# Column tiles for the SSM lag and V products and for the sample value products of the second layer

## What is computed

```python
def s5_scan(u, h0, ...):                       # layer 0, 96 groups of 16 channels, 64 states
    a_bar, b_bar = jnp.exp(lam_dt), ((a_bar - 1.0) / lam)[..., None] * bmat
    # h[t] = a_bar * h[t-1] + b_bar @ u[t];  y[t] = real(cmat @ h[t]) + d * u[t]

def stick_breaking_attention(q, k, v, q_offset):   # layer 1, 12 heads of 128
    z = jnp.einsum('bqhd,bkhd->bhqk', q_blk, k).astype(jnp.float32) * scale
    log_keep = jnp.where(causal, jax.nn.log_sigmoid(-z), 0.0)
    later = lax.cumsum(log_keep, axis=3, reverse=True) - log_keep
    w = jnp.where(causal, jnp.exp(jax.nn.log_sigmoid(z) + later), 0.0)
    return jnp.einsum('bhqk,bkhd->bqhd', w.astype(v.dtype), v)

def layer_b(x, k_all, v_all, q_offset, mk, mv, w_in, w_out, g_pre, g_post):
    q, gate, mq, mg = _split_proj(rms_norm(x, g_pre) @ w_in)
    b_out = stick_breaking_attention(...) * jax.nn.silu(gate)
    m_out = mem_attention(mq, mk, mv) * jax.nn.silu(mg)
    return x + rms_norm(jnp.concatenate([b_out, m_out], axis=-1) @ w_out, g_post)
```

## Time and profile before

| | |
|---|---|
| median of 3 runs | 2393.51 us (2393.07 to 2394.95) |
| profiled execution | 2395.48 us, span of the trace 2393.9 us |
| PE busy | 2296.2 us (96%) |
| DVE, ACT, POOL busy | 1014.2, 892.0, 237.0 us |
| chain that ended last | PE 78%, DVE 10%, DMA 4%, issue 4%, ACT 3% |

### The profile page before, as it was taken

The page is one execution under the profiler, slowest core; times in us unless marked ns, Lnnn a source line. Parts: engine busy times, 40 slices in busy tenths (PEclk is TensorE's granted clock), DMA queues, the critical chain, the costliest instruction groups (busy, mean ns, idle before and its releaser), DMA issues.

```text
span 2393.9 us, 35551 instructions
## 1 busy us (share of the span) xinstructions
PE 2296.2 (96%) x13685; PEld 2074.6 (87%) x13685; DVE 1014.2 (42%) x1775; ACT 892.0 (37%) x1637; POOL 237.0 (10%) x479
## 2 busy tenths in 40 slices
PE   8999999999799999999999999999999999889997
PEld 6799999999788998887888889988989988878886
DVE  5658877987534463225221222222211223543223
ACT  5533333334345352224222223544445444442221
POOL 1520000000101000002000000111121111010001
PEclk9999999999999999999999999999999999989999
DMA  7634453534534334224233334334343345344223
GB/s 257 219 87 103 103 110 92 115 95 99 203 115 146 106 103 167 77 73 158 93 101 101 100 93 140 103 112 138 99 132 114 103 147 197 100 144 166 79 78 133
DMA packets 197626, 293.38 MB, mean 123 GB/s; under 512 B 48324, under 2 KB 126672, under 8 KB 194096
## 3 DMA queue, kind: packets, MB, share of 16 engines
q1 hardware_dynamic: 158832, 166.80, 24.6%
q0 software_dynamic: 19856, 81.51, 10.3%
q10 hardware_dynamic: 18864, 44.05, 5.1%
HBM read 243.75 MB, written 48.55 MB: 122 GB/s over the span
## 4 chain that ended last, share of the span: by engine, by line
PE 78%; DVE 10%; DMA 4%; issue 4%; ACT 3%; POOL 0%; SPq 0%; ACTq 0%; DVEq 0%; POOLq 0%
PE PS L206 11%; PE PS L1336 11%; PE PS L1338 11%; PE PS L1337 11%; PE PS L207 11%; PE PS L208 10%; DVE WL L188 2%; PE PS L1122 1%; PE PS L489 1%; DVE FA L642 1%; DVE FA L638 1%; PE PS L792 1%; DVE FA L633 1%; PE PS L1107 1%; DVE FA L635 1%
## 5 line engine op out<-in xcount | busy, mean ns | idle before, releaser
L206 PE MATMUL PS<-XH,WH 128*128 128x320 f32 x2336 | 742.1, 318 | 3.7 <-DVE XL L1405 1.4
L207 PE MATMUL PS<-XL,WH 128*128 128x320 f32 x2336 | 725.3, 311 | 0.0
L208 PE MATMUL PS<-XH,WL 128*128 128x320 f32 x2336 | 725.0, 310 | 0.0
L188 DVE SCALAR_TENSOR_TENSOR WL<-RAW,vec,WH 128x256 fp32r<-128x256 f32 (+1 forms) x608 | 284.4, 528 | 640.5 <-ACT WH L174 636.0
L1336 PE MATMUL PS<-WH,XH 128*128 128x512 f32 x1168 | 456.5, 391 | 4.5 <-DVE WL L183 1.4
L1337 PE MATMUL PS<-WL,XH 128*128 128x512 f32 x1168 | 455.1, 390 | 0.0
L1338 PE MATMUL PS<-WH,XL 128*128 128x512 f32 x1168 | 454.9, 390 | 0.0
L206 PEld LDWEIGHTS PS<-XH,WH 128*128 128x128 f32 x2336 | 442.7, 190 | 11.9 <-issue 6.3
L207 PEld LDWEIGHTS PS<-XL,WH 128*128 128x128 f32 x2336 | 442.6, 189 | 3.1 <-issue 2.9
L208 PEld LDWEIGHTS PS<-XH,WL 128*128 128x128 f32 x2336 | 441.8, 189 | 0.0
L174 ACT ACTIVATE WH<-RAW,vec 128x256 fp32r<-128x256 f32 (+1 forms) x608 | 281.2, 532 | 380.9 <-DMA RAW<-in_w_kv_dram 177.1
(11 more groups left out here) (296 smaller groups left out, 2153.3 us busy)
## 6 DMA issues: line engine op xcount, KB each, us to landing
RAW<-in_w_in_a_dram SPq DMA_DIRECT2D x64, 512.0 KB, 3.9
RAW<-in_w_in_b_dram SPq DMA_DIRECT2D x64, 512.0 KB, 3.7
RAW<-in_w_kv_dram SPq DMA_DIRECT2D x48, 512.0 KB, 3.6
RAW<-in_w_out_a_dram SPq DMA_DIRECT2D x32, 512.0 KB, 3.9
RAW<-in_w_out_b_dram SPq DMA_DIRECT2D x32, 512.0 KB, 3.9
scratch_in_a<-EST ACTq DMA_DIRECT2D x32, 320.0 KB, 4.0
RAW<-in_w_glu_dram SPq DMA_DIRECT2D x24, 384.0 KB, 3.3
scratch_in_b<-EST ACTq DMA_DIRECT2D x26, 320.0 KB, 4.3
```

The lines of the kernel that those rows point to most:

```text
L188: ins = eng.scalar_tensor_tensor(out=wview(WL, slot, ph)[:, kt, :], in0=wview(RAW, slot, ph)[:, kt, :], scalar=vec[:, g:g + 1], in1=wview( ...
L206: pe.matmul(acc, wh, xh, start=first, stop=False)
L207: pe.matmul(acc, wh, xl, start=False, stop=False)
L208: return pe.matmul(acc, wl, xh, start=False, stop=last)
```

## The change

1. **Lag products**: pair j's 32-wide result goes to partitions 32(j mod 4) of bank 4 + j/4, so that four neighbours use four column tiles in turn. ACT copies both banks with one activation, and the store's view follows.
2. **V products**: each group's 64 states are a product of their own, 64 wide and of its own 80 columns, in two column tiles in turn; the parts use banks 4, 6 and 5, 7. The wait of the second part on the first copy goes. ACT copies a part with two activations over all partitions.
3. **Sample values of layer 1**: the weights become the stationary operand (32 tokens wide, two streams accumulated, the other stream's columns zero in `WZ`), cached values stream with 128 columns, in four column tiles. The result is token-major; ACT copies it to `OST`, PE turns it with the next head's keys, ACT copies it once more and stores it apart, at the next head's place (`sample_out`), with an extra turn and store after the loop. The exponential writes the past weights into `WZ` with two activations and the rest with one of 384 columns. The load of the heads becomes four DMAs.

```diff
                     pe.wait_ge(s_wve, i * 4 + 4)
-                else:
-                    pe.wait_ge(s_Ve, i * 2 + 1)
-                for j in range(4):
-                    jj = 4 * part + j
-                    for r in range(2):
-                        c = r * 2 * NC
-                        ins = pe.matmul(PS[:, 4 + j, c:c + 2 * NC], WV[:, (r * JB + jj) * P:(r * JB + jj + 1) * P],
-                                        U[:, 2 * jj:2 * jj + 2, :].rearrange("p q c -> p (q c)"), start=(r == 0), stop=True,
-                                        skip_group_check=True)
+                for a in range(2):
+                    for j in range(4):
+                        jj = 4 * part + j
+                        for q in range(2):
+                            c = j * NC
+                            ins = pe.matmul(PS[q * ST:q * ST + ST, 4 + 2 * a + part, c:c + NC],
+                                            WV[:, (a * JB + jj) * P + q * ST:(a * JB + jj) * P + q * ST + ST], U[:, 2 * jj + q, :],
+                                            start=(j == 0), stop=True, skip_group_check=True)
...
-                for j in range(JB):
-                    o = PS[0:32, 4 + j // 4, (j % 4) * P:(j % 4 + 1) * P]
+                for a in range(2):
                     for r in range(2):
-                        ins = pe.matmul(o, BB[:, r, j].rearrange("p q h -> p (q h)"),
-                                        CP[:, r, j, 0:8].rearrange("p k h -> p (k h)"),
-                                        start=(r == 0 and j % 4 == 0), stop=(r == 1), skip_group_check=True)
+                        for x in range(4):
+                            j = 4 * a + x
+                            ins = pe.matmul(PS[32 * x:32 * x + 32, 4 + a, 0:P], BB[:, r, j].rearrange("p q h -> p (q h)"),
+                                            CP[:, r, j, 0:8].rearrange("p k h -> p (k h)"),
+                                            start=(r == 0), stop=(r == 1), skip_group_check=True)
...
-                    for j in range(4):
-                        for q in range(2):
-                            r = slice(q * ST, q * ST + ST)
-                            ins = act.activation(W[r, :, 4 * part + j, :],
-                                                 PS[r, 4 + j, 0:320].rearrange("p (r q c) -> p r q c", r=2, q=2)[:, :, q, :], ACT.Copy)
+                    for a in range(2):
+                        ins = act.activation(W[:, a, 4 * part:4 * part + 4, :],
+                                             PS[:, 4 + 2 * a + part, 0:4 * NC].rearrange("p (j c) -> p j c", j=4), ACT.Copy)
...
+                act.activation(KDS[:], PS[:, 4:6, 0:P], ACT.Copy).then_inc(s_kde, 1)
...
                 pe.wait_ge(s_kr, h * 48 + 48)
-                pe.wait_ge(s_oe, h * 2 + 2)
+                pe.wait_ge(s_oe, h * 3 + 2)
...
+                    if x == 3:
+                        pe.wait_ge(s_zero, 4)
+                        ins = pe.transpose(PS[:, 7, P:2 * P], OST[:], ident[:])
...
-                pe.matmul(PS[:, 4, 0:P], VR[:, 4, :], WT[:, 1, 3 * P:], start=True, stop=False, **kw)
-                for b in range(NB):
-                    c = slice(DSEQ * b, DSEQ * (b + 1))
-                    ins = pe.matmul(PS[:, 4, c], VR[:, 5 + b, :], WT[:, 2, 3 * P + DSEQ * b:3 * P + DSEQ * (b + 1)],
-                                    start=False, stop=True, **kw)
+                pe.matmul(PS[:, 4, 0:P], WT[:, 1, 3 * P:], VR[:, 4, :], start=True, stop=False, **kw)
+                for a in range(2):
+                    for m in range(4):
+                        ins = pe.matmul(PS[32 * m:32 * m + 32, 4, 0:P], WZ[:, a, 32 * m:32 * m + 32], VR[:, 5 + 2 * m + a, :],
+                                        start=False, stop=(a == 1), **kw)
...
+                act.wait_ge(s_oss, h * 16 + 16)
+                act.activation(OS[:, SEQ:TOK], PS[:, 7, P:2 * P], ACT.Copy).then_inc(s_oe, 1)
+                act.wait_ge(s_oe, h * 3 + 3)
+                act.dma_start(sample_out(h, 1), OS[:, SEQ:TOK]).then_inc(s_oss, 16)
                 act.wait_ge(s_q, h * 16 + 16)
                 act.activation(QT[:], QR[:], ACT.Copy, scale=SCALE).then_inc(s_qt, 1)
...
+                act.wait_ge(s_e, h * 3 + 3)
+                past = PS[:, 6, 3 * P:].rearrange("p (m a i) -> p a m i", a=2, i=DSEQ)
+                for a in range(2):
+                    act.activation(WZ[:, a, :].rearrange("p (m a i) -> p a m i", a=2, i=DSEQ)[:, a], past[:, a], ACT.Exp)
+                act.activation(WT[:, 2, 0:3 * P], PS[:, 6, 0:3 * P], ACT.Exp).then_inc(s_w, 1)
...
-            pe.wait_ge(s_oe, 26)
+            pe.wait_ge(s_oe, 38)
+            pe.transpose(PS[:, 7, P:2 * P], OST[:], ident[:]).then_inc(s_kt, 1)
...
+            act.wait_ge(s_kt, 53)
+            act.wait_ge(s_oss, 208)
+            act.activation(OS[:, SEQ:TOK], PS[:, 7, P:2 * P], ACT.Copy).then_inc(s_oe, 1)
+            act.wait_ge(s_oe, 39)
+            act.dma_start(sample_out(BATCHES * 2, 1)[0], OS[:, SEQ:TOK]).then_inc(s_oss, 16)
...
             pool.wait_ge(s_ost, 16 * 13)
+            pool.wait_ge(s_oss, 16 * 14)
...
-                    pool.dma_start(AM[:, 6 * k:6 * k + 6, :], scr["out_b"][6 * k:6 * k + 6].rearrange("k p n -> p k n")).then_inc(s_am[k], 16)
+                    pool.dma_start(AM[:, 6 * k:6 * k + 6, 0:SEQ], scr["out_b"][6 * k:6 * k + 6, :, 0:SEQ].rearrange("k p n -> p k n")).then_inc(s_am[k], 16)
+                    pool.dma_start(AM[:, 6 * k:6 * k + 6, SEQ:], sample_out(6 * k + 1, 6).rearrange("k p n -> p k n")).then_inc(s_am[k], 16)
```

More of the change, by code:

```diff
@@ L236, in build @@
         (U, CR, SR, CTH, W, FS, FO, KDS, BVT, TZ, HPZ, PW, PB, BR, BV, TMP, CP, BB, DT, KA, DTS) = place(
-            [(2 * JB, NC), (2, P), (2 * P,), (384,), (2, JB, NC), (2, NB + 1, JB), (2 * P,), (JB, P), (2 * JB * P,),
+            [(2 * JB, NC), (2, P), (2 * P,), (384,), (2, JB, NC), (2, NB + 1, JB), (2 * P,), (2, P), (2 * JB * P,),
              (2 * JB, P), (2, 2, JB, NC), (NPW, 2, PAIRS), (NPW, 2, JB), (2, JB, GH), (2, JB, STEPS, GH),
@@ L545, in store_lags @@
                 sp.wait_ge(s_kde, i + 2)
-                dst = scr["lags"].rearrange("(x j q) h m -> x (q h) j m", j=JB, q=2)[ds(i, 1)].rearrange("o a j m -> (o a) j m")
-                sp.dma_start(dst, KDS[0:32]).then_inc(s_kst, 16)
+                dst = scr["lags"].rearrange("(x a b q) h m -> x (b q h) a m", a=2, b=4, q=2)[ds(i, 1)].rearrange("o p a m -> (o p) a m")
+                sp.dma_start(dst, KDS[:]).then_inc(s_kst, 16)
                 sp.wait_ge(s_zero, 3)
@@ L1068, in build @@
         s_kvst = [sem(f"kv_stored{t}") for t in range(NT)]
-        KR, VR, KTB, QR, QT, TP, SP_, WT, SUM1, SUM0, OS = place(
-            [(13, P), (13, P), (13, P), (TOK,), (TOK,), (3, 512), (3, 512), (3, 512), (2 * P,), (3 * P,), (TOK,)])
+        KR, VR, KTB, QR, QT, TP, SP_, WT, SUM1, SUM0, OS, WZ, OST = place(
+            [(13, P), (13, P), (13, P), (TOK,), (TOK,), (3, 512), (3, 512), (3, 512), (2 * P,), (3 * P,), (TOK,), (2, P), (P,)])
         s_q, s_qt, s_kr, s_vr = sem("q_rows"), sem("q_scaled"), sem("k_rows"), sem("v_rows")
@@ L1079, in build, with sample_out @@
         s_sp, s_spm, s_sum, s_e = sem("softplus_ready"), sem("softplus_masked"), sem("later_sums"), sem("exponent_ready")
-        s_w, s_wm, s_o, s_oe, s_ost = sem("weights_exp"), sem("weights_masked"), sem("head_product"), sem("head_copied"), sem("head_stored")
+        s_w, s_wm, s_o, s_oe, s_ost, s_oss = sem("weights_exp"), sem("weights_masked"), sem("head_product"), sem("head_copied"), sem("head_stored"), sem("head_sample_stored")
         DIAG = [(0, 0), (1, 0), (2, 0), (2, 2 * P)]
         NEW = (1, 3 * P)
+        def sample_out(k0, n):
+            v = scr["out_b"][MIXB:KT].rearrange("k p n -> (k p n)").rearrange("(x p m) -> x p m", p=P, m=P)
+            return v[ds(k0, n)].rearrange("o p m -> (o p) m") if not isinstance(k0, int) else v[k0:k0 + n]
         def sb_pe(pe, i, r):
@@ L1200, in exponential @@
                 act.wait_ge(s_o, h * 2 + 2)
-                for x in range(3):
+                act.wait_ge(s_zero, 5)
+                for x in range(2):
                     act.wait_ge(s_e, h * 3 + 1 + x)
                     act.activation(WT[:, x, :], PS[:, 4 + x, :], ACT.Exp).then_inc(s_w, 1)
+                act.wait_ge(s_e, h * 3 + 3)
[3 more added lines that the diff above has]
+                act.activation(WT[:, 2, 0:3 * P], PS[:, 6, 0:3 * P], ACT.Exp).then_inc(s_w, 1)
             def output():
@@ L1209, in output @@
                 act.wait_ge(s_o, h * 2 + 4)
-                act.activation(OS[:, SEQ:TOK], PS[:, 4, 0:P], ACT.Copy).then_inc(s_oe, 1)
-                act.wait_ge(s_oe, h * 2 + 4)
-                act.dma_start(scr["out_b"][ds(h, 1)].rearrange("o p n -> (o p) n"), OS[:]).then_inc(s_ost, 16)
+                act.activation(OST[:], PS[:, 4, 0:P], ACT.Copy).then_inc(s_oe, 1)
+                act.wait_ge(s_oe, h * 3 + 4)
```

(9 more changed lines are left out.)

## The result

The changed kernel takes 2381.5 us (median; 2376.2 to 2385.7) against 2393.3 in the same runs for the kernel before: a ratio of 0.9950, with a 95% interval of 0.9937 to 0.9963. It is faster, by 11.8 us where 26.6 was forecast, and lies above the range.

What follows compares the result with a forecast made beforehand. PE, busy 2296.2 of 2393.9 us, was taken as the bound, with other chains close behind. The SSM loop's 20.7 us and the heads' 5.9 made 26.6 off, hence 2367 us, range 2358 to 2380.

Steps and rivals of the forecast that it cites:

- The price of column tiles: Narrow tiles pay 0.34 us extra a block; V block 1.72 us instead of 2.47, lag block 1.51 instead of 4.11.
- The first rival: V products: load and product do not overlap within a tile, block 2.58 us, 2377 us in all; chance 0.15.
- The ring: SSM loop: V products, copy, 42.6 us of DVE, turn and PE up to V set the round; 3.45 us saved.
- The clock: Rival: clock drops behind PE's new waits, 1.57 us each, at up to 36 places; 17 cancel the gain; chance 0.07.
- the split: SSM loop: PE's new waits of 2.0 us a round are divided between L516 and L463.
- the bound that I had named: Sign of a wrong forecast: more than three clock drops in the SSM and stick-breaking loops.
- another sign of being wrong: Sign of a wrong forecast: DVE idles inside its chain in the SSM loop.
- the 3.5 forecast there: Gain of 3.5 us expected between the sixth V block and the first head's turn.
- The heads: Stick-breaking loop and its end: sample values 1.19 us shorter a head, limited by the keys' load; 5.9 us in sum.

## Why the prediction was wrong

- **The price of column tiles** was right: the V block 1.75 against 1.72, the lag block 1.51 as forecast. The first rival (V rounds in line, a block of 2.58) is out. The Trainium skill, "TensorE: Matmul & The Clock Gate", section on packing small matmuls, has it that a weight load overlaps a product in flight only when the row group differs; the 16 rounds of two tiles 64 wide in 1.75 us, all with the same rows, speak against it, and so do the lag tiles, even with two products of one tile in a row in the program (1.54).
- **The ring** was right: 3.42 a round, DVE without a wait on PE from first scan step to L690, the lag saving returned as waits. The lag tiles alone gave nothing, and without them the changed kernel is PE's again, at 74.29.
- **The clock** is the step that failed. Its price was right (1.57 from the earlier trace rows; 6.16 - 4.61 = 1.55 at L516, 1.45 of it in the round), its place too, but I gave it 0.07, because waits of 0.8 and 0.6 had caused no drop and the new 2.0 a round would be split in two. The rows of the SSM loop say nothing on waits beyond 0.8, the drop of the earlier trace rows itself stood behind a wait of 0.59, and the split was assumed, though the sum held it: the lag block and the V blocks lie between L463 and L516, so what PE gains there comes out at L516. It had 0.83 + 4.10 - 3.45 = 1.48 there, and 1.47 came. So five drops lay in the two loops, where three were the bound that I had named, and with each of them DVE idled inside its chain (at L706), which was another sign of being wrong: 5 x 1.45 = 7.2 of the 11.5 missing between forecast and profiled execution.
- **The rest** of the 11.5 is the prologue with 1.2, the way from the sixth V block to the first head's turn with 3.5 besides its drop, and less 0.7 gained with the heads. The prologue's 1.2 is within the spread of single executions: in the eight profiled ones with the changed SSM loop, whose code is the same up to there, the first V block starts at 177.1 to 183.8 us. Of the 3.5, 0.6 is lost up to the first memory product (66.9 us behind the sixth V block before, 65.5 now, so 3.45 - 1.45 - 1.4 = 0.6), where the wait for a load grew. Another 1.4 goes up to the next projection of the memory branch, which starts 201.1 us behind the sixth V block in both; on the way there is a half-speed stretch at 693 us that the kernel before doesn't have. The last 1.5 is lost behind that point. There a half-speed stretch stands in both (at 752.7 and 754.8 us): before, ahead of a wait for ACT that took up its cost, now behind it. The waits, before and after:

```profile
PE PS L792 <- DMA FA<-out_mem_k_prompt: 6.3, 1, 6.3
PE PS L206 <- ACT EST L1623: 0.6, 1, 0.6
...
PE PS L787 <- DMA FA<-out_mem_k_prompt: 6.8, 1, 6.8
PE PS L206 <- ACT EST L1639: 2.1, 1, 2.1
```

  What brings the stretch at 693 us is open: of the kernels with the new SSM loop only the two with idle products and the keys' load in its old place are without it. In the five such kernels whose rounds have no drop, the whole way took 924.2 to 930.4 us, before 927.4, so what is kept of the 3.5 forecast there can't be told from single executions.
- **The heads** were right in sum, 5.6 + 1.0 against 5.9, and in kind: the keys' load is late at every head (I had it at most of them, 0.3 to 1.2 each; it was at all eleven, 14.6 / 11 = 1.3). One term was off by a little: 15.80 - 15.6 leaves 0.2 us a head in five of them, not 0.1. The run with early keys shows that this load held back another 5.9. But 3 to 4 is the better figure for the step, and the profile's 5.6 was some luck.

What stays open is the border itself. Waits of 1.4 to 2.0 us at the state products cause a drop in most rounds, not in all, waits of the same length for the keys seldom do, and which are spared no run explains: with 1.47 us it was the first round in three kernels out of three, with 2.0 the last.

## What to carry to other kernels

When a ring through another engine sets the pace, cutting PE's work inside it only lengthens PE's wait; add up where that wait will stand, as one number at one place, before calling it free. If the sum passes what the trace has shown to be harmless at that place (1.0 us at the state products; another place had a drop behind 0.59), try to keep PE busy in it: one idle product of 0.43 us was worth 7 us in the rounds and 10 in the medians, and putting 2.6 us of work back into each round was worth 4 in the medians. Then follow a load that ends the wait to the queue that issues it: moving the keys' load ahead of a few masks gave 5.9 us between the first and the twelfth turn, more than the 3 to 4 of the new tiles of the values.

## What I had not expected of the hardware

- At the state products a wait of PE of 1.4 to 1.5 us was followed by 3.4 us at half the granted clock in 18 of 24 rounds, while one of 1.0 us was not in any of 12. Two of 2.0 us were followed by 6.8 us. Ahead of the keys' turn, 26 waits of 1.4 to 1.86 us were followed by none.
- A stretch of 3.4 us at 1.2 GHz costs 1.43 to 1.55 us and not more, in the round as in the block: with the lag tiles alone 78.41 - 76.98 = 1.43.
- Two fp32 products to one column tile in a row in the program, in a block that uses four tiles, take 1.54 us for 32 records, against 1.51 when the tiles take turns.
